# A Trainium2 kernel of two residual blocks: preparations woven into the gemms they feed, the 31-tap convolution laid between evictions, parts split by other engines

## What is computed

```python
def mix_stream(z, k, v, rope, g_q, w_q_b, conf_dw_w, ...):
    q = mla_queries(z[..., :Q_END], g_q, w_q_b, rope)
    attn = block_attention(q, k, v)
    conf = conformer_branch(z[..., ROPE_END:CONF_END], conf_dw_w, ...)
    sc = shortconv_branch(z[..., CONF_END:], sc_dw_w)
    merged = jnp.concatenate([rmsnorm(attn, ...), rmsnorm(conf, ...), rmsnorm(sc, ...)], axis=-1)
    return merged @ w_o

def sqrelu_mlp(h, w1, w2):
    a = jax.nn.relu(h @ w1)
    return (a * a) @ w2
...
    hl = modulate(rmsnorm(xl, g_pre_mix[i]), ml[0], ml[1])
    zl = hl @ w_in[i]
...
    xl_new = xl + ml[2] * rmsnorm(y_l, g_post_mix[i])
    h2 = modulate(rmsnorm(xl_new, g_pre_mlp[i]), ml[3], ml[4])
    xl_new = xl_new + ml[5] * rmsnorm(sqrelu_mlp(h2, w_mlp_in[i], w_mlp_out[i]), g_post_mlp[i])
...
def hybrid_layer(x, norm_g, w_in, ...):
    h = rms_norm(x, norm_g)
    proj = jnp.einsum('btd,de->bte', h, w_in)
    (qa, ka, va, za, ba, aa, ub, zb, qc, kc, vc, zc, iq, ik, iw, gates) = split_columns(proj)
    ...
    return x + jnp.einsum('btd,de->bte', merged, w_out).astype(x.dtype)
```

## Time and profile before

| what | value |
|---|---|
| median of three runs | 3333.5 us (3328.46 to 3336.76) |
| the profiled execution itself | 3320.93 us |
| its span, first to last instruction | 3319.6 us |
| mean granted TensorE clock | .951 |
| TensorE busy, matmuls | 2959.3 us, 16384 |
| VectorE, ScalarE, GpSimd busy | 1531.2, 1041.7, 1682.3 us |
| low cuts L2588 on GpSimd | 444 x 2.379 = 1053.5 us |

### The profile page before, as it was taken

One profiled execution on the slowest core, in us unless ns is written; L12 is line 12 of the kernel. 1 busy time (PEld: TensorE's weight loads), 2 busy tenths in 40 slices (PEclk: granted clock), 3 DMA queues, 4 the chain that ended last, 5 costly groups with the idle time before them and its releaser, 6 DMA issues.

```text
span 3319.6 us, 41505 instructions
## 1 busy us (share of the span) xinstructions
PE 2959.3 (89%) x16384; PEld 2412.8 (73%) x16384; DVE 1531.2 (46%) x2534; ACT 1041.7 (31%) x1702; POOL 1682.3 (51%) x1240
## 2 busy tenths in 40 slices
PE   6768888897999968898999899999889899998988
PEld 5557567786888756566888677888767778886766
DVE  3538554224122358543212356545682275446742
ACT  3233344333222332443222333222322333223331
POOL 4246226886555654335555555445525554446344
PEclk8789899998999989998999999999999999999998
DMA  7342122453333221222333222111212221112222
GB/s 287 127 158 65 56 96 81 149 165 102 95 95 96 84 91 61 77 83 65 94 102 95 74 83 73 52 57 57 71 51 76 74 89 61 52 58 64 63 66 70
DMA packets 81217, 291.71 MB, mean 88 GB/s; under 512 B 9088, under 2 KB 9344, under 8 KB 80640
## 3 DMA queue, kind: packets, MB, share of 16 engines
q1 hardware_dynamic: 81024, 289.06, 27.2%
HBM read 286.93 MB, written 2.10 MB: 87 GB/s over the span
## 4 chain that ended last, share of the span: by engine, by line
PE 67%; DVE 17%; POOL 6%; issue 4%; ACT 4%; DMA 1%; SPq 0%; ACTq 0%; POOLq 0%; DVEq 0%
PE ps L568 49%; DVE t L2033 5%; PE ps L541 5%; PE ps L694 2%; DVE t L2364 2%; POOL t L2588 1%; PE ps L596 1%; PE ps L714 1%; DMA t<-in_wmod 1%; PE ps L939 1%; PE ps L948 1%; PE ps L871 1%; PE ps L953 1%; POOL t L2781 1%; POOL t L2608 1%
## 5 line engine op out<-in xcount | busy, mean ns | idle before, releaser
L568 PE MATMUL ps<-t,t 128*128 128x512 f32 (+3 forms) x9936 | 2257.0, 386 | 129.6 <-POOL t L2588 48.4
L568 PEld LDWEIGHTS ps<-t,t 128*128 128x128 f32 x9936 | 1813.8, 193 | 501.3 <-issue 97.5
L2588 POOL TENSOR_TENSOR t<-t,t 128x1024 fp32r<-128x1024 f32 (+3 forms) x444 | 1053.5, 2379 | 684.2 <-ACT t L1227 683.1
L1227 ACT ACTIVATE t<-t 128x1024 fp32r<-128x1024 f32 (+3 forms) x444 | 458.3, 1035 | 1064.3 <-PE ps L568 1006.0
L541 PE MATMUL ps<-t,t 128*128 128x128 f32 (+2 forms) x1540 | 238.4, 293 | 151.8 <-DVE t L1812 65.7
L541 PEld LDWEIGHTS ps<-t,t 128*128 128x128 f32 (+2 forms) x1540 | 182.2, 146 | 215.6 <-DVE t L1812 48.3
L2117 DVE TENSOR_TENSOR t<-t 128x512 f32<-128x512 f32 (+1 forms) x96 | 66.0, 688 | 341.0 <-ACT t L1476 341.0
L2033 DVE SCALAR_TENSOR_TENSOR t<-t,t,t 128x512 f32<-128x512 f32 (+1 forms) x180 | 157.1, 873 | 6.4
L2781 POOL TENSOR_TENSOR t<-t,t 128x512 fp32r<-128x512 f32 (+1 forms) x96 | 127.3, 1326 | 58.4 <-DVE t L1788 55.5
L2129 DVE TENSOR_TENSOR t<-ps,t 128x512 f32<-128x512 f32 x60 | 41.0, 691 | 218.3 <-PE ps L568 218.3
L2608 POOL TENSOR_TENSOR t<-t,t 128x4 f32<-128x4 f32 (+2 forms) x93 | 88.6, 952 | 88.5 <-DVE t L1820 54.4
(11 more groups left out here) (253 smaller groups left out, 2662.2 us busy)
## 6 DMA issues: line engine op xcount, KB each, us to landing
t<-in_wbig SPq DMA_DIRECT2D x412, 512.0 KB, 3.6
t<-in_wmod SPq DMA_DIRECT2D x96, 512.0 KB, 5.8
t<-in_wbig SPq DMA_DIRECT2D x16, 416.0 KB, 3.2
t<-in_wbig SPq DMA_DIRECT2D x14, 256.0 KB, 2.8
...
```

Source lines behind the costliest of these rows:

```text
L568: m = p.matmul(out, lhs, rhs, start=kk == 0 and n == 0, stop=kk == tiles - 1 and n == 2)
L1227: a.activation(c.hi(w), c.raw(w), ACT.Copy).then_inc(w_hi.h, w_hi.up(("cut", w)))
L2588: g.tensor_tensor(c.lo(w), c.raw(w), c.hi(w).bitcast(F32), ALU.subtract).then_inc(w_lo.h, w_lo.up(("cut", w)))
```

## The change

1. **Woven preparations.** In c0, l0, mc0, l1, ml1, d0 and d1 the first gemm starts after the steps for tile 0, and the rest of the preparation is woven into it, one step a k-tile. In l0 and mc0 the residual of the mix before comes at the preparation's end (`then`). The hybrid layers do qa first, then sm.
2. **Parts.** The high part is a copy by ScalarE, the low part a subtraction by VectorE, for all nine preparations (72 tiles).
3. **c1 and l1.** The first steps of l1's preparation stand inside c1, between zt, zT and kv; c1's kv uses four banks.
4. **Convolution.** The 62 instructions are yielded one by one and woven into zt, sc and sb at 1.3 (c0) or 1.4 a step; what is left comes after sb.
5. **Perceptron residuals.** Y times gain is done when a block is complete (`gained`), and the residual is one instruction a block.
6. **mc0's low part** `bl` moves to VectorE, right behind `bh`.

The instructions of TensorE stay 13,942 by the program; ScalarE's go from 1461 to 1533, VectorE's from 2438 to 2480, GpSimd's from 1236 to 1132.

```diff
+def then(steps, work, *args):
+    yield from steps
+    work(*args)
...
     def prepared(n):
-        return lambda k: ((dve, ("ph", n, k)), (pool, ("pl", n, k)))
+        return lambda k: ((act, ("ph", n, k)), (dve, ("pl", n, k)))
...
     def layer(i):
-        yield from prep(f"d{i}")
+        first = onward(prep(f"d{i}"), 5)
         ready = prepared(f"d{i}")
+        yield from weave(delta_in(i, ("qa",)), first, 0.5)
         yield from product_gemm(("sm", i), "TM", (c.AH, c.AL), 512, 332, 8, ready, lambda b: ((act, ("sm", i, b)),))
-        yield from delta_in(i)
+        yield from delta_in(i, ("ka", "va", "za"))
...
     run(mods(0, 0, 4, main))
-    run(g)
-    run(weave(mix("c0"), mods(0, 4, 6, main), 0.06))
+    onward(g, 3)
+    run(weave(weave(mix("c0"), mods(0, 4, 6, main), 0.06), g, 0.5))
...
     run(weave(project("c0"), both(rest, g, 4), 0.4))
-    run(g)
-    run(mix("l0"))
+    next(g)
+    run(weave(mix("l0"), g, 0.5))
...
-    run(g)
-    run(mlp("mc0", prep("ml0"), 0.8))
+    next(g)
+    run(weave(mlp("mc0", prep("ml0"), 0.8), g, 0.5))
     run(mlp("ml0", prep("c1"), 0.4))
-    run(mix("c1"))
-    run(prep("l1"))
-    run(mix("l1"))
+    keys = onward(mix("c1"), 9)
+    g = onward(prep("l1"), 4)
+    next(keys)
+    next(g)
+    run(keys)
+    run(weave(mix("l1"), g, 0.5))
...
-    run(prep("ml1"))
-    run(mlp("ml1", iter(()), 0.0))
+    g = onward(prep("ml1"), 5)
+    run(weave(mlp("ml1", iter(()), 0.0), g, 0.5))
...
+        def high(k):
+            A.wait_ge(act, ("pe", n, k))
+            a.activation(c.AH[:, k, 0:T], TM[:, 512 * (k % 2):512 * (k % 2) + T], ACT.Copy).then_inc(
+                act.h, act.up(("ph", n, k)))
...
         for k in range(8):
-            V.wait_ge(act, ("pe", n, k))
-            v.tensor_copy(c.AH[:, k, 0:T], c.TM[scratch][:, 512 * (k % 2):512 * (k % 2) + T]).then_inc(
-                dve.h, dve.up(("ph", n, k)))
+            V.wait_ge(act, ("ph", n, k))
+            v.tensor_tensor(c.AL[:, k, 0:T], c.TM[scratch][:, 512 * (k % 2):512 * (k % 2) + T],
+                            c.AH[:, k, 0:T].bitcast(F32), ALU.subtract).then_inc(dve.h, dve.up(("pl", n, k)))
...
         if row is not None:
-            V.wait_ge(act, ("row", n))
+            for t in range(nt - 1):
+                gained(n, 1, t)
         V.wait_ge(act, ("ysq", n, 1, nt - 1))
...
+        if row is not None:
+            gained(n, 1, nt - 1)
+            V.wait_ge(dve, ("yg", n, 1, nt - 1))
         V.wait_ge(pool, ("rr", n))
         for t in range(nt):
-            if row is None:
-                v.scalar_tensor_tensor(x[:, t, :], y[:, t, :], r[:, t:t + 1], x[:, t, :], ALU.mult,
-                                       ALU.add).then_inc(dve.h, dve.up(("x", n, t)))
-            else:
-                v.scalar_tensor_tensor(y[:, t, :], y[:, t, :], r[:, t:t + 1], row, ALU.mult, ALU.mult).then_inc(
-                    dve.h, dve.up(("yr", n, t)))
-                V.wait_ge(dve, ("yr", n, t))
-                v.tensor_tensor(x[:, t, :], x[:, t, :], y[:, t, :], ALU.add).then_inc(dve.h, dve.up(("x", n, t)))
+            v.scalar_tensor_tensor(x[:, t, :], y[:, t, :], r[:, t:t + 1], x[:, t, :], ALU.mult, ALU.add).then_inc(
+                dve.h, dve.up(("x", n, t)))
...
+            taps, rate = conv(), 1.4 if nt == 4 else 1.3
             yield from product_gemm(("cf", n), 4, 8, cf)
-            conv()
-        yield from product_gemm(("zt", n), nt, 8, lambda b: None)
-        if not short:
-            yield from product_gemm(("sc", n), 4, 8, sc)
+            yield from weave(product_gemm(("zt", n), nt, 8, lambda b: None), taps, rate, finish=False)
+            yield from weave(product_gemm(("sc", n), 4, 8, sc), taps, rate, finish=False)
...
             high(c.BH[n][:, kk, :], q[:, :], ("bh", n, g, kk))
+            if n == "mc0":
+                V.wait_ge(dve, ("bh", n, g, kk))
+                v.tensor_tensor(c.BL[n][:, kk, :], q[:, :], c.BH[n][:, kk, :].bitcast(F32), ALU.subtract).then_inc(
+                    dve.h, dve.up(("bl", n, g, kk)))
...
-    run(g)
-    residual("c0")
+    next(g)
+    run(weave(mix("l0"), then(g, residual, "c0"), 0.5))
```

More of the change, by code:

```diff
@@ L1296, in prep @@
         yield 0
+        if read:
+            A.wait_ge(gemm, ("end", read))
+        high(0)
         for k in range(8):
+            if k < 7:
+                high(k + 1)
             if k < 6:
@@ L1443, in mix @@
                     act.h, act.up(("q", n, t)))
+        if short:
+            yield
         for t in range(nt):
@@ L2549, in dve_program @@
     run(weave(project("l0"), both(rest, g, 4), 0.4))
-    run(g)
-    residual("l0")
-    run(mlp("mc0", prep("ml0"), 0.8))
+    next(g)
+    run(weave(mlp("mc0", prep("ml0"), 0.8), then(g, residual, "l0"), 0.5))
     residual("mc0")
@@ L3000, in pool_program @@
     run(weave(project("l0"), both(rest, steps, 4), 0.4))
-    run(steps)
-    residual("l0")
-    run(mlp("mc0", prep("ml0"), 0.8))
+    next(steps)
+    run(weave(mlp("mc0", prep("ml0"), 0.8), then(steps, residual, "l0"), 0.5))
     residual("mc0")
```

173 lines of the change are left out of this document (102 added, 71 removed).

## The result

The changed kernel takes 3287.7 us (median of four runs, 3283.0 to 3290.9), the kernel before, measured beside it, 3331.8: ratio .9865, interval .9845 to .9885, 44 us. The prediction was 3296 (3274 to 3322). Between the two profiled executions the difference is 38.0 us, 3281.6 against 3319.6 of span; the prediction had 37.8 for these.

What follows compares the result with a forecast made beforehand. TensorE was taken as the bound, with only its 360 us of idle time to win; the stage gains summed to 37.8 us, taking the 3333.5 us median to 3296 us, range 3274 to 3322.

Steps and rivals of the forecast that it cites:

- c0: Mix c0: q and kv run beside the last 22 taps, VectorE ends last, attention starts at 116; gain 10.8 us (7 to 12).
- l0: Mix l0: gemm cf starts earlier, but c0's residual now stands before the taps on VectorE; gain .5 us (-2 to +3).
- Weaving: Stage starts: first gemm starts after turns 0 to 4, three turns inside it; 2.8 us in ml1, 2.7 in d1.
- The charge of .8 us a stage for the clock: Woven first gemms in ml1, d0, d1: starting nearer the idle stretch, at half clock, was charged .8 us each.
- d0 and d1: Hybrid layers, to gemm ub: woven preparation in both, one-instruction residual ahead of d0; gains 6.3 us (5 to 8) and 2.7 (1.5 to 3.5).
- late next is the square sum and mean: Entry of d0: after the residual, the next late thing is the square sum and mean, which no edit touches; no separate size.
- c1 and l1: l1's first steps fill the wait inside c1, so l1's cf starts 7.5 us earlier; gain 6.5 us (4 to 9).
- ml0's and c1's preparations: Preparations hidden in mc0's last w2 and in ml0: less port work shrinks waits; gains 6 us (3 to 9) and .7.
- 34.5 without the 8 subtractions: ml0's preparation in mc0's last w2: VectorE and GpSimd work falls from 44.3 to 34.5 us in 41.8 us.
- the other argument, which wait comes next: mc0's groups 1 to 3: a wait of some 4 us at tile 7 replaces 2.8 at w2's start; gain 0 (-12 to +12).
- The slower one: Rival, woven gemms: the preparation chain becomes the pace, 64 us lost over 7 preparations, 3360 us; chance .07.
- The condition that I named: Woven gemms: the slower case decides from a chain above 5.5 us; with scaling and subtraction each waiting for a cut, 7.8 us.

Runs made afterwards that it cites:

- x_sm_first: Against x_cast_all: in the hybrid layers the preparation is woven into sm, with sm ahead of qa as in the kernel before; 3274.0 us, ratio to before .9830.
- x_cast_dve: Against the changed kernel: in ml0's and c1's preparations the high part is VectorE's cast again, the low part stays VectorE's subtraction; 3293.6 us.
- x_cast_all: Against the changed kernel: in all nine preparations the high part is VectorE's cast, the low part VectorE's subtraction; 3280.5 us, ratio to before .9847.

## Why the prediction was right, point by point

- **Sum and size: right.** 44 us against 37.8, and 3287.7 us lies in the range (3274 to 3322) and in the forecast's own (3286 to 3308); between the profiled executions 38.0. That the sum comes out to .2 us there is luck: single terms differ from mine by up to 7 us, and they cancel.
- **c0: right in place, sized high.** v at 116.7 (said 116); q no longer waits, VectorE ends last. The gain was 9.0 for 10.8, and 2.4 of it is a different start of the run: the first turn came at 35.44 instead of 37.87, and at 37.24 in the second execution of the changed kernel. That leaves 6.6.
- **l0: sized low,** 3.5 for .5. From c0's end to the end of sb it takes 93.5 us before, 90.1 after and 93.1 with the weaving undone: the residual of c0 between cf and the taps did not take back what the earlier gemm gave.
- **Weaving: right in place, sized low.** Gemms start 5.2 to 5.4 us after the first turn (said 5.7). The charge of .8 us a stage for the clock had the wrong sign in ml1: half-clock time from the wait to the end of w1's first gemm fell from 17 to 10 us. The Trainium skill (TensorE: Matmul & The Clock Gate, "HAM oscillation — how this bites in real kernels") says that idle gaps bring the throttle back and that each costs a slow stretch. The section is about waits longer than the 1.4 us between turns, so the .8 that I paid for closing these was a step of mine. Its sign is right in ml1; what closing them alone gives, no run shows.
- **d0 and d1: mis-sized**, 4.2 and 1.1 for 6.3 and 2.7. The turns of d0 do start 3.5 us earlier after ml1. But from first turn to za's end it takes 115.4 us in both layers, where it took 115.5 and 115.7: the weaving was to give 2.8 and 2.7 there. The step that failed is "late next is the square sum and mean": the exchange of qa and sm put a wait of 3.3 us into va, and I had not costed that exchange at all. x_sm_first takes it out, and the stretch falls to 110.6 and 109.5.
- **c1 and l1: mis-sized**, 13.3 for 6.5. The sum counted the order and weaving; the one-instruction residual was costed only for ml1's, ahead of d0, though ml0's gives 3.5 here, and the shorter preparation only in the hidden ones. The term had a slip too: 7.5 less 1.3 for turns and .5 for half clock is 5.7, not 6.5.
- **ml0's and c1's preparations: wrong.** I divided SBUF work by time (44.3 to 34.5 us in 41.8) and took 6 + .7; it was 1.2 and -3.4. The step that failed is "34.5 without the 8 subtractions": they left GpSimd but came to VectorE. GpSimd's work in ml0's stretch did fall from 27.9 to 18.1 us, but VectorE's rose from 16.4 to 27.7, and the sum is 45.8. 9.3 us of the rise are the parts: eight casts of 5.5 us in all gave way to eight subtractions of 14.8, of which five take 2.4 us and more, beside a low cut. The rest is mostly mc0's low part and the gain products, which moved here too. The subtractions:

```profile
L1866 DVE TENSOR_TENSOR t<-t,t 128x512 fp32r<-128x512 f32 x8 | 14.8, 1854 | 7.6 <-ACT t L1294 7.5
```

On top comes the order in the queues, where ScalarE's new copy stands behind a cut that waits for a slot. With VectorE's cast in its place (x_cast_dve) the two preparations are 2.9 and 2.2 us shorter. In mc0's groups the other argument, which wait comes next, held: 3.4 to 3.7 us at tile 7 for a forecast of some 4. The three groups lost 2.1 us (said 0), with 6.8 us more at half clock.

- **The rivals.** The slower one was real, and I gave .07 for a reason that was half right. The condition that I named (a chain over 5.5 us for two k-tiles) is reached with the subtraction on GpSimd, by standing behind the cut rather than by taking turns at the port. The rule on the port (the Trainium skill, SBUF — State Buffer, "Who interferes with whom": the one that issues second waits for the whole instruction of the other) holds in these traces: .69 us alone, 2.4 beside a cut. But at most one of a tile's VectorE instructions meets a cut (x_cast_all at the entry of ml1).
- **Left out:** half of the gain lies in TensorE's busy time, through the clock, and the sum had next to no term for it. 4.3 us of it are the net of the three stretches that no edit touched (-7.0, 5.5 and 5.8 in the table); why the half-clock stretches left or came there is open.
